# Splitting the first gather of each layer by expert pairs in a one-core backbone kernel

## The reference, cut to what matters

```python
def expert_choice_ffn(h, w_router, w1, w3, w2):
    B, n, _ = h.shape
    cap = EC_FACTOR * n // N_EXPERTS
    aff = jax.nn.softmax((h @ w_router).astype(jnp.float32), axis=-1)
    g, idx = lax.top_k(jnp.swapaxes(aff, 1, 2), cap)
    ...
    xs = h[bidx, idx]
    hid = jax.nn.silu(jnp.einsum('becd,edf->becf', xs, w1)) * jnp.einsum('becd,edf->becf', xs, w3)
    y = jnp.einsum('becf,efd->becd', hid, w2) * g[..., None].astype(h.dtype)
    return jnp.zeros_like(h).at[bidx, idx].add(y)
```

## Time and profile before

| | us |
|---|---|
| three runs, median (lowest to highest) | 1829.0 (1826.6 to 1829.05) |
| profiled execution, its own time | 1829.94 |
| its span | 1828.1 |
| PE matmul busy | 1607.3 (88%) |
| PE weight load busy | 935.0 (51%) |
| DVE / ACT / POOL busy | 634.2 / 341.5 / 248.7 |
| HBM read | 527.48 MB, mean 289 GB/s |

### The profile page before, as it was taken

How to read it: one execution, slowest core, us unless ns; L and a number is a source line. 1 busy time by engine, 2 the same in 40 slices (tenths; PEclk the granted TensorE clock), 3 DMA queues, 4 the chain that set the end, 5 groups by cost and what they waited for, 6 DMA issues and landing times.

```text
span 1828.1 us, 23593 instructions
## 1 busy us (share of the span) xinstructions
PE 1607.3 (88%) x9789; PEld 935.0 (51%) x9789; DVE 634.2 (35%) x1194; ACT 341.5 (19%) x871; POOL 248.7 (14%) x282
## 2 busy tenths in 40 slices
PE   7999999999999989989899899999998676675666
PEld 3656466677785423424222587779975222232222
DVE  1865346587753212122020455353232010110101
ACT  3223344111122100100001422442220000000001
POOL 4102221344211000000100001224500000000000
PEclk9999999999999999999999999999999877787778
DMA  9525005264696999999999644233798999999996
GB/s 354 195 92 170 1 1 185 92 211 157 228 396 258 421 421 421 421 421 421 412 421 421 254 173 116 89 116 114 267 368 341 421 421 421 421 421 420 420 421 272
DMA packets 135794, 530.11 MB, mean 290 GB/s; under 512 B 10229, under 2 KB 74907, under 8 KB 81161
## 3 DMA queue, kind: packets, MB, share of 16 engines
q1 hardware_dynamic: 132904, 525.23, 72.6%
q0 software_dynamic: 2784, 3.38, 0.9%
HBM read 527.48 MB, written 1.09 MB: 289 GB/s over the span
## 4 chain that ended last, share of the span: by engine, by line
PE 62%; DMA 31%; DVE 4%; issue 1%; ACT 1%; SPq 0%; DVEq 0%; ACTq 0%
DMA ring<-in_w_e_dram 30%; PE ps L1052 12%; PE ps L1409 12%; PE ps L1682 10%; PE ps L1515 5%; PE ps L1461 4%; PE ps L1708 4%; PE ps L950 2%; PE ps L1615 2%; PE ps L1340 2%; PE ps L1247 2%; PE ps L1643 1%; PE ps L1362 1%; PE ps L1125 1%; DMA ring<-in_w_mod_dram 1%
## 5 line engine op out<-in xcount | busy, mean ns | idle before, releaser
L1682 PE MATMUL ps<-ring,arena 128*32 128x256 f32 (+1 forms) x2840 | 372.4, 502 | 106.4 <-DMA ring<-in_w_e_dram 103.4
L1682 PEld LDWEIGHTS ps<-ring,arena 128*32 128x32 f32 (+1 forms) x2840 | 123.5, 128 | 337.0 <-DMA ring<-in_w_e_dram 159.6
L1708 PE MATMUL ps<-ring,arena 128*32 128x256 f32 (+1 forms) x1480 | 206.7, 545 | 66.9 <-DMA ring<-in_w_e_dram 65.3
L1708 PEld LDWEIGHTS ps<-ring,arena 128*32 128x32 f32 (+1 forms) x1480 | 67.0, 137 | 201.7 <-issue 104.6
L2658 DVE COPY arena<-ps 32x512 f32<-32x512 f32 (+1 forms) x124 | 68.6, 553 | 277.9 <-PE ps L1708 276.6
L1763 ACT ACTIVATE arena<-ps 128x256 f32<-128x256 f32 (+6 forms) x226 | 96.5, 437 | 292.8 <-PE ps L1409 168.4
L2095 ACT ACTIVATE arena<-ps 128x512 f32<-128x512 f32 (+1 forms) x32 | 15.7, 490 | 721.9 <-PE ps L1682 721.9
L2651 DVE TENSOR_TENSOR arena<-arena,ps 128x512 f32<-128x512 f32 (+1 forms) x32 | 17.7, 554 | 373.4 <-PE ps L1682 373.4
L1052 PE MATMUL ps<-arena,ring 128*128 128x512 f32 (+1 forms) x416 | 141.5, 496 | 0.0
L1409 PE MATMUL ps<-arena,ring 128*128 128x128 f32 (+1 forms) x672 | 117.0, 321 | 0.0
L1409 PEld LDWEIGHTS ps<-arena,ring 128*128 128x128 f32 x672 | 101.0, 191 | 16.5 <-issue 9.6
(11 more groups left out here) (276 smaller groups left out, 1826.1 us busy)
## 6 DMA issues: line engine op xcount, KB each, us to landing
ring<-in_w_e_dram SPq DMA_DIRECT2D x361, 1024.0 KB, 15.3
ring<-in_w_in_dram SPq DMA_DIRECT2D x42, 1024.0 KB, 10.4
ring<-in_w_mod_dram SPq DMA_DIRECT2D x32, 1024.0 KB, 7.9
arena<-in_w_e_dram SPq DMA_DIRECT2D x17, 1024.0 KB, 8.1
ring<-in_w_mod_dram SPq DMA_DIRECT2D x16, 512.0 KB, 10.5
ring<-in_w_out_dram SPq DMA_DIRECT2D x8, 1024.0 KB, 9.9
arena<-in_w_mod_dram SPq DMA_DIRECT2D x8, 1024.0 KB, 15.0
arena<-in_w_br_ml_dram SPq DMA_DIRECT2D x8, 512.0 KB, 6.5
```

The source lines that it names most:

```text
L1682: mm = pe.matmul(ps[M * j:M * j + M, m, 0:NW], XSTs[l][e // GROUP % 2][:, kk, e % GROUP, 0:M], w[:, k, j * NW:(j + 1) * NW], start=kk == 0 ...
L1708: mm = pe.matmul(ps[M * j:M * j + M, 3, 0:NW], lhs, w[:, k, j * NW:(j + 1) * NW], start=kk == 0, stop=kk == KD - 1)
```

## The change

The first gather of a layer is made in two calls. `FIRST_TWO` makes the rows of experts 0 and 1 before the loop, with 64 moving columns instead of 128; `LAST_TWO` makes those of experts 2 and 3 after `expert_in(0, 1)`, with 64 columns too. The weights of each matmul are the same 128 x 128 blocks in both calls. The first call waits for 2 scaled one-hots rather than 4 (in layer 0 the other two are waited for at the latent piece). ACT and DVE take the two halves in two passes of narrower operations, the second behind `silu` and `hid` of expert 0. `expert_in(2, 0)` waits for the second half. Counts of the semaphores `gathered`, `xs_lat` and `xs_ctx` follow. No load is moved.

```diff
+FIRST_TWO, LAST_TWO = slice(0, 2), slice(2, GROUP)
...
-                def gather(g, pieces):
-
-                    pe.wait_ge(sem("rows_scaled"), before("rows_scaled", l) + 2 * L.ns * (g + 1))
+                def gather(g, pieces, es=slice(0, GROUP)):
+
+                    pe.wait_ge(sem("rows_scaled"), before("rows_scaled", l) + (2 * L.ns * (g + 1) if g else 2))
+                    if g == 1:
+                        pe.wait_ge(sem("xs_lat"), before("xs_lat", l) + 4)
+                        if L.ns == 2:
+                            pe.wait_ge(sem("xs_ctx"), before("xs_ctx", l) + 4)
                     if g >= 2:
                         pe.wait_ge(sem("ya_added"), before("ya_added", l) + 1 + NB_ * (g - 1))
                     for b, si in pieces:
                         s = L.streams[si]
                         if l == 0 and g == 0 and s:
                             pe.wait_ge(sem("mod_row"), 5)
+                            pe.wait_ge(sem("rows_scaled"), 4)
                         for i in range(4):
                             k = 4 * b + i
                             for c2 in range(2):
-                                mm = pe.matmul(ps[:, 4 + 2 * s + b, i * P:(i + 1) * P], X[:, 2 * s + c2, paired(k)],
-                                               Srs[l][:, si, c2, :], start=c2 == 0, stop=c2 == 1)
+                                mm = pe.matmul(ps[:, 4 + 2 * s + b, i * P + CAP * es.start:i * P + CAP * es.stop], X[:, 2 * s + c2, paired(k)],
+                                               Srs[l][:, si, c2, CAP * es.start:CAP * es.stop], start=c2 == 0, stop=c2 == 1)
...
-                        if e % GROUP == 0 and m == 0:
-                            x_at = 2 * (e // GROUP) + q // 2 + 1
+                        if (e % GROUP == 0 or e == 2) and m == 0:
+                            x_at = 2 * (e // GROUP) + (2 if e else 0) + q // 2 + 1
...
-                gather(0, gather_pieces(L, 0))
+                gather(0, gather_pieces(L, 0), FIRST_TWO)
...
+                    if e == 0:
+                        gather(0, gather_pieces(L, 0), LAST_TWO)
...
-                                act.wait_ge(sem("gathered"), before("gathered", l) + 2 * L.ns * g)
+                                act.wait_ge(sem("gathered"), before("gathered", l) + 2 * L.ns * (g + 1))
...
-                def gathered_ctx(g):
+                def gathered_ctx(g, es=slice(0, GROUP)):
 
                     for k in range(KD):
                         b, i = divmod(k, 4)
                         if i == 0:
-                            act.wait_ge(sem("gathered"), gathered_by(L, g, b, 0))
-                        ins = act.activation(XSTs[l][g % 2][:, k, :, 0:CAP],
-                                             ps[:, 4 + b, i * P:(i + 1) * P].rearrange("p (e j) -> p e j", e=GROUP),
+                            act.wait_ge(sem("gathered"), gathered_by(L, g, b, 0, es))
+                        ins = act.activation(XSTs[l][g % 2][:, k, es, 0:CAP],
+                                             ps[:, 4 + b, i * P + CAP * es.start:i * P + CAP * es.stop].rearrange("p (e j) -> p e j", j=CAP),
...
-                    gathered_ctx(0)
+                    gathered_ctx(0, FIRST_TWO)
...
+                    if e == 0 and L.ns == 2:
+                        gathered_ctx(0, LAST_TWO)
...
-                def gathered_lat(g):
+                def gathered_lat(g, es=slice(0, GROUP)):
 
                     for k in range(KD):
                         b, i = divmod(k, 4)
                         if i == 0:
-                            dve.wait_ge(sem("gathered"), gathered_by(L, g, b, ns - 1))
-                        ins = dve.tensor_scalar(XSTs[l][g % 2][:, k, :, (ns - 1) * CAP:ns * CAP],
-                                                ps[:, 6 + b, i * P:(i + 1) * P].rearrange("p (e j) -> p e j", e=GROUP),
+                            dve.wait_ge(sem("gathered"), gathered_by(L, g, b, ns - 1, es))
+                        ins = dve.tensor_scalar(XSTs[l][g % 2][:, k, es, (ns - 1) * CAP:ns * CAP],
+                                                ps[:, 6 + b, i * P + CAP * es.start:i * P + CAP * es.stop].rearrange("p (e j) -> p e j", j=CAP),
...
-                gathered_lat(0)
+                gathered_lat(0, FIRST_TWO)
...
+                    if e == 0:
+                        gathered_lat(0, LAST_TWO)
...
-def gathered_by(L, g, b, si):
-
-    return before("gathered", L.n) + 2 * L.ns * g + gather_pieces(L, g).index((b, si)) + 1
+def gathered_by(L, g, b, si, es):
+
+    return before("gathered", L.n) + 2 * L.ns * (g + (1 if g or es.start else 0)) + gather_pieces(L, g).index((b, si)) + 1
```

More of the change, by code:

```diff
@@ L99 @@
     x_post1=4, x_post2=4, logit_parts=2, lgT_ready=2, logits=2, logits_used=4, lg_shift=1, lg_exp=1, aff_ready=1, affT_tr=1, rank_ready=1, rank_tr=1,
-    hot_ready=16, rows_scaled=16, weighted=4, gathered=16, gt_tr=4, gt_ready=4, xs_lat=8, xs_ctx=8, silu=N_EXP,
+    hot_ready=16, rows_scaled=16, weighted=4, gathered=20, gt_tr=4, gt_ready=4, xs_lat=10, xs_ctx=10, silu=N_EXP,
     hid_ready=N_EXP, hid_tr=N_EXP, hidT_ready=N_EXP, y_taken=N_EXP,
@@ L1623, in turn_gates @@
                         pe.wait_ge(sem("g2_taken"), before("g2_taken", l) + 2 * L.ns)
-                    last = 2 * min(g + 2, GROUPS)
+                    last = 2 * min(g + 2, GROUPS) + 2
                     pe.wait_ge(sem("xs_lat"), before("xs_lat", l) + last)
```

## The result

The changed kernel takes 1833.09 us (median of 7 runs, 1832.19 to 1836.21) against 1828.75 us (7 runs, 1826.6 to 1829.34): a ratio of 1.003, 95% interval 1.0018 to 1.0041. It is 3.3 to 7.5 us slower by the interval, 4.3 us by the medians. The profiled execution has a span of 1831.3 us, 3.2 above that of before.

What follows compares the result with a forecast made beforehand. Transfers were taken to bound layer 0's expert stage. Layer 0 +4.5 us and layer 1 0 gave 1834.4 us from the profiled 1829.94, or 1833.5 from the 1829.0 median; range 1830.0 to 1837.5 for 8 in 10.

Steps and rivals of the forecast that it cites:

- The gather's own length: Layer 0's first gather: weight loads set the pace, so each 64-column half takes 7.8 us, like the whole before.
- The start: Layer 0's first gather waits for 2 of 4 scalings and so begins 0.5 us earlier (0 to 0.6).
- The block and the reserve: Layer 0 behind expert 0: second half makes PE 7.3 us late, the load queue nearly empties, transfers lose 4.5 us.
- The load of 622.58: Layer 0 load issued then in the kernel before, 9.1 us to landing; forecast to go at 629.9, queue about empty.
- the first drain: Queue draining at layer 0's second half by 1 to 2 us, counted as part of the 4.5 us, not on top.
- The price of the restart: Layer 0 loads into an empty queue: the first takes 4.9 us to land, the second 7.0.
- Layer 1: Its second half's 3.9 us of PE behind expert 0 is hidden by existing waits for loads; cost 0.
- The reserve of 7 us: Layer 1's load queue: the load at 1385.21 took 14.0 us, less 7.0, leaving 7 us of reserve.
- A reserve that covers it: Rival, chance 0.25: layer 0 loses only 2 to 3.6 us; time 1831.5 us.
- A gather of half the length: Rival, chance 0.06: moving columns set the pace, a half takes 3.5 us; time 1822.5 us, faster.
- A longer block: Rival, chance 0.09: second half meets a wait or drains add up, layer 0 loses 6 to 7; time 1835.5 us.
- a further debt at the drain: Second mechanism of the longer rival: each of two drains leaves its own debt, 1 to 2 us, then 4.4 later.

Runs made afterwards that it cites:

- the block of 128 columns: Kernel before plus 64-instruction-long idle gather matmuls behind expert 0 in layer 0, 128 moving columns instead of 64; one run, layer 0 stage 439.3 us.
- the five kernels with one whole block: The change, its split in layer 0 alone, and the kernel before plus idle second-half matmuls (64 columns, 128 columns, weight step of one); mean layer 0 stage 439.5 us.
- the four with an untouched layer 0: The kernel before, the split only in layer 1, tripled idle matmuls in layer 1, and only the eased start wait; mean layer 0 stage 434.4 us.
- the triple block: Kernel before plus 48 idle matmuls behind expert 0 in layer 1, three times the second half; ratio 1.0026 (1.0015 to 1.0036).
- layer 1 alone: The change with the gather split only in layer 1, layer 0 as in the kernel before; ratio 1.0012 (1.0003 to 1.0021).
- the block alone: Kernel before plus 32 idle matmuls like the second half, behind expert 0 in layer 0, nothing else changed; ratio 1.0045 (1.0033 to 1.0058).
- the double block: Kernel before plus 64 idle matmuls behind expert 0 in layer 0, twice the second half; ratio 1.0068 (1.0052 to 1.0083).

## Why the prediction was right, and where it wasn't

**The gather's own length: right.** 7.75 us for 64 columns, forecast 7.8. The run of 16 columns in the earlier trace rows was the row that decided, and the block of 128 columns shows it from the other side. The table by moving columns alone in the Trainium skill, "TensorE: Matmul & The Clock Gate", section "Back-to-back issue gap", is given there for a matmul by itself. It doesn't describe fp32 matmuls with a new 128-column weight each: 0.12 us an instruction at 64 and at 128 columns.

**The start: right.** 0.59 us, forecast 0.5.

**The block and the reserve: right in kind and place.** PE behind it was late by 7.1 us, counted from L956's start, forecast 7.3. The load of 622.58 was the one at which the reserve ended. Its successor landed 74.6 us behind L956's start, 70.4 before: 4.2 late, forecast 4.4. That the first drain, at 595 us, is contained in the second and not added is borne out too: the load of 595.62 landed 1.2 us late by the same count, and the one at 628.86 4.2. The price of the restart holds over the five kernels with one whole block: there the load of 622.58 took 4.9 to 5.2 us to land in four and 6.2 in the change itself (forecast 4.9), and the second, whose lateness stays, 6.4 to 7.2 (forecast 7.0).

**What the sum left out.** The load at 632.30 lost 1.3 us more, and layer 0 ended 5.2 us late by that count (1004.19 - 562.96 against 999.82 - 563.79), 0.7 above the 4.5. The term that these two profiles make too small is the layer's loss to the block: 4.5 forecast, 5.2 measured. But 0.7 us is inside the noise of the measure, and the profile before is its shortest. The means of the five profiles with a whole block and of the four with an untouched layer 0 lie 5.1 us apart; less 0.6 for the start that is the 4.5 of the forecast. What fits the 1.3 us is below.

**Layer 1: 0, right as far as the traces show.** The load issued at 1393.59, the first behind the block, took 9.1 us to land (14.0 before), so nothing ran dry. Layer 1's stage cost nothing in either profile with a split there, and three times the block cost it 2.5 us. The reserve of 7 us was sized too small, without effect on the sum: a load that took 14.0 us wasn't behind a full queue (those from 1390 on took 16.7), and behind the triple block the first two loads took 5.4 and 7.0 us where they had taken 14.0 and 16.2, which is a reserve of 8.6 to 9.2. The runs of layer 1 alone leave a possible 0.5 us and more unexplained.

**The total.** Forecast 1833.5, measured 1833.1 (4.3 us slower by the medians, 3.3 to 7.5 by the interval, forecast 4.5). The layer's 5.2 us showed as 3.2 in the profiled spans, since that execution was 0.8 us ahead before the change's place and lost 0.9 less in layer 1's loads and 0.3 less in the tail. The nearness of the median is partly luck of that size.

**The rivals.** A reserve that covers it falls with the block alone and the double block. A gather of half the length falls with the timeline. A longer block didn't happen. Its second mechanism, a further debt at the drain, would be near the 0.7 us, but nothing shows it beyond the noise.

## What to carry to other kernels

An fp32 matmul of up to 128 moving columns with a fresh 128-column weight has a floor set by the weight load: cutting the moving operand of such a product in two doubles its price and shortens nothing. If it must be cut, cut along the axis that divides the weight loads; here that avoided the loss, and gained nothing that the runs can tell. Where a transfer queue bounds the stage, PE time is free up to the queue's reserve and costs about one for one behind it. The reserve is read where the time to landing is shortest, from the load after that one: its time less what the second load into an empty queue takes, 9.9 - 7.0 = 2.9 us in layer 0 and 16.2 - 7.0 = 9.2 in layer 1, against about 2.6 and 9 measured. An earlier restart is worth only what the second, third and fourth load gain with it.

## What the runs showed of the hardware

**The second load pays more than the first.** A 1 MB load took 4.8 to 5.2 us into an empty queue in the thirteen profiles (the first after the gather of layer 0), 2.5 of which are its transfer at full rate. The next, issued 1.7 us behind it, took 5.9 to 7.2. A predecessor that is nearly done doesn't always cost that much: with 0.3 to 1.6 us of it left, the load of 622.58 took 4.9 to 5.2 us in four kernels with the block; with 2.0 left it took 6.2 in the change.

**An instruction packet can cost the loads a microsecond.** The DMA view counts the packets of an instruction queue among those of the core's 16 engines. In the changed kernel from 637.8 to 639.8 us, between the two landings that lie 1.3 us too far apart, it has one (queue, packets, MB, share of the engines' time), and the loads beside it:

```profile
q8 instruction: 1, 0.02, 2.9%
ring<-in_w_e_dram SPq DMA_DIRECT2D x2, 1024.0 KB, 8.7
```

Landings 3.5 to 3.8 us apart instead of 2.5 followed such a packet at 593, 614 and 638.5 us in this kernel. In the kernel before the packets at 598 and 622 us cost 0.2 us each and the one at 648 nothing, yet one at 827 us was followed by a landing 3.7 us behind its predecessor. A short queue isn't needed for it: that load had taken 16.6 us, and in the split of layer 1 alone, with a packet at 622.0, this one landed at 625.5, 3.8 us behind its predecessor:

```profile
609.07 0.33 SPq L565 DMA_DIRECT2D ring<-in_w_e_dram  x1
ring<-in_w_e_dram SPq DMA_DIRECT2D x1, 1024.0 KB, 16.5
```

That one landing, 1.3 us late, accounts for the +1.2 us of its layer 0 stage; so such packets make at least a part of the noise of the stage measure. At 638 to 640 us a landing 2.8 to 3.9 us behind its predecessor followed the packet in all five kernels with one whole block, and none in the four with an untouched layer 0, whose packet comes at 645 to 648. Whether the drained queue or the moment of the packet makes that difference, and what decides the price of a packet, stays open.

**PE's clock in the mixer isn't steady.** Between the layers, 1030 to 1370 us, the granted clock is 0.99 in the profile before, 0.98 in that of layer 1 alone:

```profile
1030.00:1370.00 340.00, 327.18 (x2013) 0.99 0.50 172
```

```profile
1030.00:1370.00 340.00, 328.56 (x2010) 0.98 0.49 169
```

In the latter profile this stage is 1.8 us longer with the same code. From 1036 to 1043 us its granted clock is 0.54 with PE at work, near the lower level of 1.2 GHz, after PE had stood idle for 2.15 us up to 1035.9; before has 1.00 there. Both profiles fall to the lower level once more for 3 us at about 1195 to 1200. In the thirteen profiles the stage took 370.9, 372.5 or about 374.5 us, and the four long ones have about 10 us at the lower level in it, the others 3 to 7. Such a step explains a part of the spread of the runs, and is a reason to compare stages and not spans. The comparison of before and after is free of it: the stage took 372.5 us in both.
